# Parameters of a recurrence loaded as contiguous rows and turned into columns by TensorE, and x asked for ahead of the broadcast rows

## The chip, the cores and the metric

One core of a Trainium2 chip runs one program. The metric is the time of the whole program on the device in microseconds (us); lower is better. The kernel before takes 2596.82 us, the median of three runs.

## The reference

Two transformer blocks are computed one after the other for one sequence of 256 tokens with width 1024. The first has three parts that matter here:

```python
ada = silu(c) @ ada_w + ada_b                 # 1024 -> 6144: shifts, scales, gates
h = rms_norm(x, mix_pre_g) * (1 + sc_m) + sh_m
u_s, q, k, v, g_s, g_a = split(h @ w_in)

# the recurrence: 32 groups of 16 channels, 64 complex states each
dt = exp(log_dt)[:, None];  lam_bar = exp(lam * dt)          # lam, dt: (32, 64)
b_bar = ((lam_bar - 1) / lam)[..., None] * b_mat             # (32, 64, 16)
bu = einsum('gpc,sgc->sgp', b_bar, u);  states = scan(lam_bar, bu)
y = einsum('gcp,sgp->sgc', c_mat, states).real + d_skip * u
```

Attention, a mixture of 32 experts and the second block (which also reads a memory whose norm has the gain `mem_norm_2`) follow.

## The kernel before

The kernel is written out by hand for each engine. Every engine has its own program of stages (`pe_s0`, `pe_s1`, ... for TensorE; the same for ScalarE `act_`, VectorE `dve_`, GpSimd `pool_` and SyncE `sp_`) that it runs strictly in order; semaphores connect them. What matters here is stage 0.

**Weights** come through SyncE's DMA queue into a ring of six slots of 2 MB (`RING`, `stream`, L302). The first six pieces are the first half of `ada_w` (1024 x 512 each), then four pieces of `w_in`, then the rest of `ada_w`. `sp_first` asks for c, for the constants `k_main` (identity, masks, tables), for six pieces, and, after waits on `ssm_in` and `rope_in`, for the following ones. From the seventh piece on each waits until TensorE has used the slot.

**Small data** comes through GpSimd's DMA queue (`pool_s0`, L346). The recurrence wants its parameters as columns: state (g, s) of a group pair on one of 128 partitions, the 16 pairs j along the free dimension. So `ssm_lam_re`, `ssm_lam_im` and `ssm_log_dt` (twice) are read by a rearranging access pattern, one 4-byte word at a time; `ssm_d` and `mem_norm_2` likewise; `ssm_b` in runs of 16 words, `ssm_c` in runs of 64 words. Behind these come `positions` spread to all partitions, the table `k_hot` and `rel_bias_2`, then x (1 MB), three rows of `ada_b` and two gains, each spread to 128 partitions (0.5 MB each).

**ScalarE and VectorE** (`act_s0`, `dve_s0`) make silu(c), the rotary tables, and from the parameters `lam_bar` and `bbar`, which is multiplied into block-diagonal masks `Bd` and `Cd`; VectorE then waits (L481) until all six `ada_w` pieces are through TensorE and makes shift, scale and gate (L482 to L486) and h (L572, L573).

**TensorE** (`pe_s0`) waits for silu(c), multiplies it with the six pieces in their order (L507; eight matmuls of 128x128 by 128x512 for a piece, into banks 0 to 5), computes a bias table (`pe_bias`, L335) in bank 7, and transposes `Bd` and `Cd` (L520) into banks 6 and 7. Then it turns h (L553) and starts the projections (L583). A float32 matmul shows as two records in the trace, a transpose as one.

Of the kernel before, what the change touches and what calls it, by code (L numbers as in the profile page):

```python
# [7 lines left out]
P = 128  # L8
# [3 lines left out]
KD = D // P  # L12
# [6 lines left out]
SQ = SW // P  # L19
# [82 lines left out]
def block_kernel(nc, A, out, names):  # L102
# [39 lines left out]
    with ctx:  # L142
# [15 lines left out]
        def ar(at, n, rows=P):  # L158
            return AR[0:rows, at:at + n]
# [76 lines left out]
        def ar3(at, n, k):  # L236
            return ar(at, n).rearrange("p (k m) -> p k m", k=k)
# [11 lines left out]
        braw = [ar3(10240 + 256 * n, 256, SJ) for n in range(2)]  # L249
# [96 lines left out]
        def pool_s0(pool):  # L346
            for s, a in ((lam_re, "ssm_lam_re"), (lam_im, "ssm_lam_im")):
                dma(pool, s, A[a][0].rearrange("(j g) s -> (g s) j", g=2), par_in)
            for g in range(2):
                src = A["ssm_log_dt"][0]  # L350
                dma(pool, dt_c[g * SSM_P:(g + 1) * SSM_P, :],
                    bass.AP(src.tensor, src.offset + g, [[0, SSM_P], [2, SJ]]), par_in)
            for n, a in enumerate(("ssm_b_re", "ssm_b_im")):
                dma(pool, braw[n], A[a][0].rearrange("(j g) s c -> (g s) j c", g=2), ssm_in)
            for n, a in enumerate(("ssm_c_re", "ssm_c_im")):
                dma(pool, craw[n], A[a][0].rearrange("(q r) c s -> (r c) q s", q=SQ), ssm_in)
            dma(pool, dcol, A["ssm_d"][0].rearrange("(q p) -> p q", p=P), ssm_in)
            dma(pool, sinR.bitcast(i32), row(A["positions"][0]), rope_in)
            pool_bias_loads(pool)
            dma(pool, mem_g, A["mem_norm_2"].rearrange("i (k p) -> p i k", p=P), mem_in)  # L360
            dma(pool, x3, A["x"][0].rearrange("(t p) d -> p t d", p=P), x_in)
            for n, d in enumerate((shm, Am, GTm)):
                dma(pool, d, row(A["ada_b"][0][n * D:(n + 1) * D]), mod_in)
            dma(pool, gpre, row(A["mix_pre_g"][0]), mod_in)
            dma(pool, gpost, row(A["mix_post_g"][0]), mod_in)

        def sp_first(sp):

            dma(sp, c_col, A["c"].rearrange("a (k p) -> p (a k)", p=P), c_in)
            dma(sp, CON[:, :], A["k_main"], con_in)  # L370
            stream(sp, 0, SLOTS)
            sp.wait_ge(ssm_in, 16 * 5)
            sp.wait_ge(rope_in, 16)
            stream(sp, SLOTS, FIRST)

        def act_s0(act, o):
            act.wait_ge(c_in, 16)
            o(act.activation(cond, c_col, ACT.Silu), cond_silu)
            act.wait_ge(par_in, 16 * 4)
            o(act.activation(dt_c, dt_c, ACT.Exp), par_exp)  # L380
            act.wait_ge(par_red, 1)
            o(act.activation(mag, mag, ACT.Exp), par_exp)
            act.wait_ge(par_red, 2)
# [8 lines left out]
            for n in range(4):  # L392
                act.wait_ge(bc_ps, n + 1)
                o(act.copy(BC[n], bank(6 + n % 2).rearrange("p (q m) -> p q m", q=SQ)), bc_ev)
# [17 lines left out]
        def dve_s0(dve, o):  # L412
# [4 lines left out]

            dve.wait_ge(rope_in, 16)
# [43 lines left out]
            dve.wait_ge(ssm_in, 16 * 5)  # L462
# [25 lines left out]
        def dve_tables(dve, o):  # L488

            dve.wait_ge(bc_ps, 4)  # L490
# [19 lines left out]
        def pe_s0(pe):  # L510
            pe.wait_ge(cond_ready, 1)
            pe_ada(pe, pc_ada, 0)
            pe_bias(pe)
            for n in range(4):
                pe.wait_ge(bc_ready, n + 1)
                if n >= 2:
                    pe.wait_ge(bc_ev, n - 1)
                src = (Bd + Cd)[n]
                for q in range(SQ):
                    m = pe.transpose(bank(6 + n % 2)[:, q * P:(q + 1) * P], src[:, q * P:(q + 1) * P], ident)  # L520
                m.then_inc(bc_ps, 1)
# [396 lines left out]
        def act_s5(act, o):  # L918
            act_turned(act, o, mgT, "merged")
            act.wait_ge(mem_in, 32)  # L920
# [1258 lines left out]
```

## Time and profile before

| | |
|---|---|
| median of three runs | 2596.82 us (2589.68 to 2599.2) |
| profiled execution, its own time | 2604.98 us |
| span of the profiled execution | 2603.2 us |
| TensorE matmul busy | 2217.3 us (85% of the span), 9934 records |
| VectorE / ScalarE / GpSimd busy | 25% / 14% / 4% |
| mean granted TensorE clock | 0.928 |
| DMA | 580.81 MB, mean 223 GB/s |

The rows further down come from one profiled execution. Times count from the start of its span. "Idle before <- releaser" says how long an engine had done nothing and what ended that. A DMA's "us to landing" counts from the start of its issue. The granted clock is a share of TensorE's full speed, 2.4 GHz; 0.50 is 1.2 GHz. A row with x and a number merges so many records.

### The profile page before, as it was taken

What the parts mean: (1) busy time and instruction counts of PE and PEld (TensorE: products, weight loads), DVE (VectorE), ACT (ScalarE), POOL (GpSimd) and SP (SyncE); (2) the same over time, 40 slices, a digit from 0 to 9 for tenths busy, and PEclk for the clock granted to TensorE, in tenths of its full rate; (3) what the DMA queues carried; (4) which work ended last, traced back from release to release, by engine and by line L of the source; (5) the groups of instructions that cost most, each with busy time, mean ns of one, the idle gap of its engine ahead of it and who ended that gap; (6) DMA issues with size and microseconds to landing.
All of it is one profiled execution on the core that took longest, in us unless ns stands there. A gap on an engine that the chain in (4) does not pass through costs nothing.

```text
span 2603.2 us, 24334 instructions
## 1 busy us (share of the span) xinstructions
PE 2217.3 (85%) x9934; PEld 1222.6 (47%) x9935; DVE 649.2 (25%) x995; ACT 357.7 (14%) x548; POOL 108.2 (4%) x117
## 2 busy tenths in 40 slices
PE   2888689889879999997999887699979776867998
PEld 1554246333223333332333264388638575836873
DVE  2557814111111111110111124200014555421000
ACT  1111011111011111110111111100012221121000
POOL 2000001000000000000000100110000031300000
PEclk9998799999989999998999988899989888888999
DMA  9752235799589999967999862234343300013430
GB/s 224 283 208 78 89 138 228 327 390 428 238 344 428 428 428 428 427 277 329 394 428 427 331 245 81 81 114 145 131 159 102 125 1 1 1 42 115 151 113 16
DMA packets 106898, 580.81 MB, mean 223 GB/s; under 512 B 7123, under 2 KB 8163, under 8 KB 82112
## 3 DMA queue, kind: packets, MB, share of 16 engines
q1 hardware_dynamic: 101008, 562.40, 54.3%
q0 software_dynamic: 5808, 17.19, 2.8%
q8 instruction: 67, 1.10, 0.2%
q14 instruction: 15, 0.12, 0.0%
HBM read 578.49 MB, written 1.07 MB: 223 GB/s over the span
## 4 chain that ended last, share of the span: by engine, by line
PE 70%; DMA 12%; DVE 12%; ACT 4%; issue 3%; SPq 0%; DVEq 0%; another core or an unknown queue 0%; POOL 0%; ACTq 0%
PE ps L1176 15%; PE ps L1482 12%; DMA ring<-in_w_up 10%; PE ps L1192 7%; PE ps L1493 6%; PE ps L583 6%; PE ps L591 5%; PE ps L507 2%; PE ps L1200 2%; DMA ring<-in_ada_w 2%; PE ps L1827 1%; PE ps L1833 1%; PE ps L804 1%; PE ps L1166 1%; PE ps L1837 1%
## 5 line engine op out<-in xcount | busy, mean ns | idle before, releaser
L1176 PE MATMUL ps<-ring,arena 128*64 128x512 f32 x1632 | 365.5, 601 | 43.1 <-issue 30.6
L1482 PE MATMUL ps<-arena,ring 128*128 128x256 f32 x1408 | 308.4, 383 | 1.5 <-ACT arena L560 1.5
L1482 PEld LDWEIGHTS ps<-arena,ring 128*128 128x128 f32 x1408 | 270.2, 192 | 39.7 <-ACT arena L560 2.3
L1176 PEld LDWEIGHTS ps<-ring,arena 128*64 128x64 f32 x1632 | 115.4, 138 | 289.2 <-issue 258.5
L1192 PE MATMUL ps<-ring,arena 128*64 128x512 f32 x1088 | 243.4, 600 | 7.6 <-ACT arena L1135 7.6
L1108 DVE TENSOR_SCALAR arena<-ps 128x512 f32<-128x512 f32 x34 | 23.5, 692 | 614.4 <-PE ps L1176 614.4
L1493 PE MATMUL ps<-ring,arena 128*128 128x512 f32 x352 | 151.4, 592 | 0.0
L583 PE MATMUL ps<-arena,ring 128*128 128x256 f32 x672 | 148.9, 384 | 0.7 <-ACT arena L560 0.7
L1192 PEld LDWEIGHTS ps<-ring,arena 128*64 128x64 f32 x1088 | 75.6, 138 | 152.1 <-issue 137.8
L1176 PE MATMUL ps<-arena 128*64 128x512 f32 x544 | 126.3, 619 | 15.0 <-issue 15.0
L583 PEld LDWEIGHTS ps<-arena,ring 128*128 128x128 f32 x672 | 129.0, 193 | 20.3 <-issue 1.5
L591 PE MATMUL ps<-ring,arena 128*128 128x512 f32 x288 | 130.8, 615 | 3.3 <-ACT arena L1929 2.0
L1493 PEld LDWEIGHTS ps<-ring,arena 128*128 128x128 f32 x352 | 66.9, 190 | 83.3 <-issue 83.2
L553 PE MATMUL ps<-constants,arena 128*128 128x128 f32 x128 | 25.6, 377 | 78.3 <-DVE arena L1439 68.4
L591 PEld LDWEIGHTS ps<-ring,arena 128*128 128x128 f32 x288 | 56.4, 197 | 74.4 <-issue 69.9
L1512 DVE TENSOR_TENSOR arena<-arena,ps 128x512 f32<-128x512 f32 x22 | 15.1, 688 | 302.5 <-ACT arena L1504 302.5
L1176 PEld LDWEIGHTS ps<-arena 128*64 128x64 f32 x544 | 39.2, 142 | 100.3 <-issue 99.5
L507 PE MATMUL ps<-ring,arena 128*128 128x512 f32 x96 | 46.5, 648 | 46.4 <-DMA ring<-in_ada_w 46.4
L1110 DVE TENSOR_SCALAR arena<-ps 128x512 f32<-128x512 f32 x34 | 23.5, 692 | 226.4 <-PE ps L1176 226.4
L1131 ACT ACTIVATE arena<-arena 128x512 f32<-128x512 f32 x34 | 21.5, 632 | 365.9 <-DVE arena L1108 365.9
L532 DVE TENSOR_SCALAR smalls<-smalls 128x2 f32<-128x2 f32 x13 | 2.6, 202 | 266.5 <-ACT arena L526 266.5
L1146 PE MATMUL ps<-arena 128*64 128x512 f32 x280 | 67.9, 606 | 0.0
(445 smaller groups left out, 2166.4 us busy)
## 6 DMA issues: line engine op xcount, KB each, us to landing
ring<-in_w_up SPq DMA_DIRECT2D x64, 2048.0 KB, 17.4
ring<-in_w_down SPq DMA_DIRECT2D x64, 2048.0 KB, 16.6
ring<-in_w_gate SPq DMA_DIRECT2D x32, 2048.0 KB, 14.0
arena<-in_w_gate SPq DMA_DIRECT2D x32, 2048.0 KB, 14.5
ring<-in_ffn_w_gate_up SPq DMA_DIRECT2D x22, 2048.0 KB, 7.9
ring<-in_ada_w SPq DMA_DIRECT2D x12, 2048.0 KB, 19.6
ring<-in_ffn_w_down SPq DMA_DIRECT2D x10, 2048.0 KB, 7.8
ring<-in_w_in SPq DMA_DIRECT2D x8, 2048.0 KB, 19.8
```

The costliest lines, as they stand in the source:

```text
L507: m = pe.matmul(bank(base + n), condrep[:, k, :], w[:, k, :], start=(k == 0), stop=(k == KD - 1))
L583: m = pe.matmul(bank(b0 + c // 2)[:, (c % 2) * SEQ:(c % 2 + 1) * SEQ], w[:, k, c * P:(c + 1) * P], src3[:, k, :], start=(k == 0), stop=(k ...
L591: m = pe.matmul(bank(banks[t]), src3[:, k, t * P:(t + 1) * P], w[:, k, :], start=(k == 0), stop=(k == kn - 1))
L804: m = pe.matmul(bank(b0 + 2 * t + c), src[:, k, t * P:(t + 1) * P], w[:, k, c * 512:(c + 1) * 512], start=(k == 0), stop=(k == 3))
L1146: m = pe.matmul(bank(2)[c * CAP:(c + 1) * CAP, :], Psel[:, t, :], h2[:, t, c * 512:(c + 1) * 512], start=(t == 0), stop=(t == 1))
L1166: pe.matmul(bank(i)[c * CAP:(c + 1) * CAP, :], Ee[odd][i * E:(i + 1) * E, :], bgu[i * E:(i + 1) * E, c * 512:(c + 1) * 512], start=True, s ...
L1176: m = pe.matmul(bank(i)[c * CAP:(c + 1) * CAP, :], xT[:, j * P + h * CAP:j * P + (h + 1) * CAP], w[h][:, j, c * 512:(c + 1) * 512], start= ...
L1192: m = pe.matmul(bank(2)[d * CAP:(d + 1) * CAP, :], actT[:, j * P + h * CAP:j * P + (h + 1) * CAP], down_w[h][:, j, d * 512:(d + 1) * 512], ...
L1200: m = pe.matmul(bank(4 + 2 * t + d), pwT[d * CAP:(d + 1) * CAP, t * P:(t + 1) * P], Yb[d * CAP:(d + 1) * CAP, :], start=False, stop=False, ...
L1482: m = pe.matmul(bank(b0 + g)[:, c * SEQ:(c + 1) * SEQ], w[:, k, (2 * g + c) * P:(2 * g + c + 1) * P], hT2[:, k, :], start=(k == 0), stop=( ...
L1493: m = pe.matmul(bank(2 * t + d), actF[:, f, t * P:(t + 1) * P], w[:, j, d * 512:(d + 1) * 512], start=(f == 0), stop=(f == FC2 - 1))
L1827: m = pe.matmul(bank(b)[:, j * P:(j + 1) * P], scr[:, m_, :], TTm[:, m_, :], start=True, stop=True)
```

## The change

The parameters `lam_re`, `lam_im`, `ssm_d` and `mem_norm_2` are loaded as rows of 128 words into 16, 16, 4 and 16 partitions of one area (`prow`), `log_dt` as 16 rows of two words (`dtrow`), which VectorE widens to rows of 128. TensorE transposes the 68 rows by 128 at once into a corner of bank 6, and VectorE copies the columns to where the kernel before had them. `ssm_b` is loaded as 16 rows of 2048 words for the real and the imaginary part; TensorE turns each of the 16 channels by a transpose of 16 x 128, for both 32 transposes, into banks 6 and 7, where VectorE reads them in place of `braw`. They stand on TensorE between the second and the third piece of `ada_w`. `positions` and x are asked for ahead of `k_hot`; waits are renumbered.

```diff
--- before.py
+++ after.py
@@ -246,7 +246,10 @@
         cosS, sinS = ar3(10240, 4096, SJ), ar3(14336, 4096, SJ)
         BTr, BTi, CTr, CTi = (ar3(18432 + 512 * n, 512, SQ) for n in range(4))
 
-        braw = [ar3(10240 + 256 * n, 256, SJ) for n in range(2)]
+        brow = [ar(14336 + 2048 * n, 2048, SJ) for n in range(2)]
+        PR = {"lam_re": 0, "lam_im": SJ, "dt": 2 * SJ, "d": 3 * SJ, "mem_g": 3 * SJ + SQ}
+        PROWS = 3 * SJ + SQ + 2 * KD
+        prow, dtrow = ar(11008, P, PROWS), AR[PR["dt"]:PR["dt"] + SJ, 11136:11138]
         bbar = [ar3(10752 + 256 * n, 256, SJ) for n in range(2)]
         craw = [ar3(11264 + 256 * n, 256, SQ) for n in range(2)]
         btmp = ar3(11776, 256, SJ)
@@ -344,21 +347,18 @@
 
 
         def pool_s0(pool):
-            for s, a in ((lam_re, "ssm_lam_re"), (lam_im, "ssm_lam_im")):
-                dma(pool, s, A[a][0].rearrange("(j g) s -> (g s) j", g=2), par_in)
-            for g in range(2):
-                src = A["ssm_log_dt"][0]
-                dma(pool, dt_c[g * SSM_P:(g + 1) * SSM_P, :],
-                    bass.AP(src.tensor, src.offset + g, [[0, SSM_P], [2, SJ]]), par_in)
+            for n, a in (("lam_re", "ssm_lam_re"), ("lam_im", "ssm_lam_im")):
+                dma(pool, prow[PR[n]:PR[n] + SJ, :], A[a][0].rearrange("(j g) s -> j (g s)", g=2), par_in)
+            dma(pool, dtrow, A["ssm_log_dt"][0].rearrange("(j g) -> j g", g=2), par_in)
+            dma(pool, prow[PR["d"]:PR["d"] + SQ, :], A["ssm_d"][0].rearrange("(q p) -> q p", p=P), par_in)
+            dma(pool, prow[PR["mem_g"]:PR["mem_g"] + 2 * KD, :], A["mem_norm_2"].rearrange("i (k p) -> (i k) p", p=P), par_in)
+            dma(pool, sinR.bitcast(i32), row(A["positions"][0]), rope_in)
             for n, a in enumerate(("ssm_b_re", "ssm_b_im")):
-                dma(pool, braw[n], A[a][0].rearrange("(j g) s c -> (g s) j c", g=2), ssm_in)
+                dma(pool, brow[n], A[a][0].rearrange("(j g) s c -> j (g s c)", g=2), ssm_in)
             for n, a in enumerate(("ssm_c_re", "ssm_c_im")):
                 dma(pool, craw[n], A[a][0].rearrange("(q r) c s -> (r c) q s", q=SQ), ssm_in)
-            dma(pool, dcol, A["ssm_d"][0].rearrange("(q p) -> p q", p=P), ssm_in)
-            dma(pool, sinR.bitcast(i32), row(A["positions"][0]), rope_in)
+            dma(pool, x3, A["x"][0].rearrange("(t p) d -> p t d", p=P), x_in)
             pool_bias_loads(pool)
-            dma(pool, mem_g, A["mem_norm_2"].rearrange("i (k p) -> p i k", p=P), mem_in)
-            dma(pool, x3, A["x"][0].rearrange("(t p) d -> p t d", p=P), x_in)
             for n, d in enumerate((shm, Am, GTm)):
                 dma(pool, d, row(A["ada_b"][0][n * D:(n + 1) * D]), mod_in)
             dma(pool, gpre, row(A["mix_pre_g"][0]), mod_in)
@@ -369,18 +369,18 @@
             dma(sp, c_col, A["c"].rearrange("a (k p) -> p (a k)", p=P), c_in)
             dma(sp, CON[:, :], A["k_main"], con_in)
             stream(sp, 0, SLOTS)
-            sp.wait_ge(ssm_in, 16 * 5)
+            sp.wait_ge(ssm_in, 16 * 4)
             sp.wait_ge(rope_in, 16)
             stream(sp, SLOTS, FIRST)
 
         def act_s0(act, o):
             act.wait_ge(c_in, 16)
             o(act.activation(cond, c_col, ACT.Silu), cond_silu)
-            act.wait_ge(par_in, 16 * 4)
+            act.wait_ge(par_red, 1)
             o(act.activation(dt_c, dt_c, ACT.Exp), par_exp)
-            act.wait_ge(par_red, 1)
+            act.wait_ge(par_red, 2)
             o(act.activation(mag, mag, ACT.Exp), par_exp)
-            act.wait_ge(par_red, 2)
+            act.wait_ge(par_red, 3)
             o(act.activation(lbi, frq, ACT.Sin, scale=TWO_PI))
             o(act.activation(lbr, tc, ACT.Sin, scale=TWO_PI), par_trig)
             act.wait_ge(rope_red, 1)
@@ -390,7 +390,7 @@
             act_rms(act, o, [x3[:, t, :] for t in range(TT)], hT[:, 0:4, :].rearrange("p k m -> p (k m)"), 1)
             act_bias(act, o)
             for n in range(4):
-                act.wait_ge(bc_ps, n + 1)
+                act.wait_ge(bc_ps, n + 3)
                 o(act.copy(BC[n], bank(6 + n % 2).rearrange("p (q m) -> p q m", q=SQ)), bc_ev)
 
         def act_tables(act, o, h):
@@ -415,6 +415,13 @@
             o(dve.tensor_copy(condrep, cols_bc(cond, P)))
             o(dve.tensor_copy(cond32, cols_bc(cond, 32)), cond_ready)
 
+            dve.wait_ge(par_in, 16 * 5)
+            o(dve.tensor_copy(prow[PR["dt"]:PR["dt"] + SJ, :].rearrange("j (g s) -> j g s", g=2), cols_bc(dtrow, SSM_P)), bc_ready)
+            dve.wait_ge(bc_ps, 1)
+            prT_ = bank(6)[:, SJ * SSM_C:SJ * SSM_C + PROWS]
+            o(dve.tensor_copy(sm(16, 3 * SJ), prT_[:, 0:3 * SJ]), par_red)
+            o(dve.tensor_copy(dcol, prT_[:, PR["d"]:PR["d"] + SQ]))
+            o(dve.tensor_copy(sm(1136, 2 * KD), prT_[:, PR["mem_g"]:PR["mem_g"] + 2 * KD]), bc_ready)
             dve.wait_ge(rope_in, 16)
             dve.wait_ge(con_in, 16)
             o(dve.tensor_copy(cosR, sinR.bitcast(i32)))
@@ -459,7 +466,9 @@
             o(dve.tensor_tensor(tc2, lbr, lam_im, ALU.mult))
             o(dve.tensor_tensor(ci, ci, tc2, ALU.subtract))
             o(dve.tensor_tensor(ci, ci, den, ALU.mult))
-            dve.wait_ge(ssm_in, 16 * 5)
+            dve.wait_ge(bc_ps, 2)
+            dve.wait_ge(ssm_in, 16 * 4)
+            braw = [bank(6 + n)[:, 0:SJ * SSM_C].rearrange("p (c j) -> p j c", c=SSM_C) for n in range(2)]
             crb, cib = cols_bc(cr, SSM_C), cols_bc(ci, SSM_C)
             o(dve.tensor_tensor(bbar[0], braw[0], crb, ALU.mult))
             o(dve.tensor_tensor(btmp, braw[1], cib, ALU.mult))
@@ -487,7 +496,7 @@
 
         def dve_tables(dve, o):
 
-            dve.wait_ge(bc_ps, 4)
+            dve.wait_ge(bc_ps, 6)
             steps = spread(con("steps"), [0, 4], [1, SEQ])
             for h in range(4):
                 f3, t3 = sinS[:, 4 * h:4 * h + 4, :], cosS[:, 4 * h:4 * h + 4, :]
@@ -508,11 +517,23 @@
                 m.then_inc(ada_ps, 1)
 
         def pe_s0(pe):
+            pe.wait_ge(con_in, 16)
+            pe.wait_ge(bc_ready, 1)
+            pe.transpose(bank(6)[:, SJ * SSM_C:SJ * SSM_C + PROWS], prow, ident[0:PROWS, 0:PROWS]).then_inc(bc_ps, 1)
             pe.wait_ge(cond_ready, 1)
-            pe_ada(pe, pc_ada, 0)
+            pe_ada(pe, pc_ada[0:2], 0)
+            pe.wait_ge(ssm_in, 16 * 4)
+            pe.wait_ge(bc_ready, 2)
+            for n in range(2):
+                by_c = brow[n].rearrange("j (s c) -> j c s", c=SSM_C)
+                for c in range(SSM_C):
+                    m = pe.transpose(bank(6 + n)[:, c * SJ:(c + 1) * SJ], by_c[:, c, :], ident[0:SJ, 0:SJ])
+            m.then_inc(bc_ps, 1)
+            pe_ada(pe, pc_ada[2:6], 2)
+            pe.wait_ge(bc_ready, 3)
             pe_bias(pe)
             for n in range(4):
-                pe.wait_ge(bc_ready, n + 1)
+                pe.wait_ge(bc_ready, n + 3)
                 if n >= 2:
                     pe.wait_ge(bc_ev, n - 1)
                 src = (Bd + Cd)[n]
@@ -917,7 +938,7 @@
 
         def act_s5(act, o):
             act_turned(act, o, mgT, "merged")
-            act.wait_ge(mem_in, 32)
+            act.wait_ge(mem_in, 16)
             act_rms(act, o, [mem_nat[:, t, :] for t in range(TT)], ar(10240, D), 2)
             act_turned(act, o, mem_T[0], "memory")
             act.wait_ge(out_ps, 5)
```

## Rows read from the trace of the kernel before

**Rows 1.** The page's chain that ended last, by line.

```profile
PE ps L1176 15%; PE ps L1482 12%; DMA ring<-in_w_up 10%; PE ps L1192 7%; PE ps L1493 6%; PE ps L583 6%; PE ps L591 5%; PE ps L507 2%; PE ps L1200 2%; DMA ring<-in_ada_w 2%; PE ps L1827 1%; PE ps L1833 1%; PE ps L804 1%; PE ps L1166 1%; PE ps L1837 1%
```

**Rows 2.** The chain in order of time, 0 to 420 us: start, us, what.

```profile
1.84 42.44 DMA ring<-in_ada_w
44.41 10.15 PE ps L507 x16
...
56.59 36.31 PE ps L507 x80
...
107.19 44.06 PE ps L583 x192
```

**Rows 3.** Timeline, 92 to 104 us: start, us, instruction, idle before.

```profile
93.02 1.22 DVE L482 TENSOR_TENSOR arena<-arena,ps 128x1024 f32<-128x1024 f32 x1 [35.73 <-PE ps L507]
...
95.81 1.09 PE L520 MATMUL ps<-constants,arena 128*128 128x128 f32 x8 [1.96 <-ACT arena L343]
...
97.26 0.42 PEld L520 LDWEIGHTS ps<-constants,arena 128*128 128x128 f32 x4 [0.59 <-issue]
...
101.91 1.97 PE L553 MATMUL ps<-constants,arena 128*128 128x128 f32 x8 [3.37 <-DVE arena L573]
```

**Rows 4.** Windows of the start: busy us by engine, PEclk, DMA share, GB/s.

```profile
9.00:18.00 9.00, 0.00 (x0) 0.00 (x0) 0.00 (x0) 0.00 (x0) 7.24 (x12) 1.00 0.98 6
18.00:22.00 4.00, 0.00 (x0) 0.00 (x0) 0.00 (x0) 0.00 (x0) 0.00 (x0) 1.00 1.73 38
22.00:29.00 7.00, 0.00 (x0) 0.00 (x0) 0.00 (x0) 0.00 (x0) 0.00 (x0) 1.00 0.31 85
29.00:38.00 9.00, 0.00 (x0) 0.00 (x0) 0.00 (x0) 1.50 (x2) 0.00 (x0) 1.00 1.14 214
38.00:45.00 7.00, 0.59 (x1) 0.50 (x2) 5.91 (x24) 1.14 (x2) 0.00 (x0) 1.00 1.03 378
```

**Rows 5.** DMA issues, 0 to 150 us: count, KB each, us to landing.

```profile
constants<-in_k_main SPq DMA_DIRECT2D x1, 1265.0 KB, 7.5
...
x_res<-in_x POOLq DMA_DIRECT2D x1, 1024.0 KB, 32.2
...
arena<-in_mix_post_g POOLq DMA_DIRECT2D x1, 512.0 KB, 39.5
...
arena<-in_ssm_b_im POOLq DMA_DIRECT2D x1, 128.0 KB, 25.7
...
arena<-in_ssm_c_im POOLq DMA_DIRECT2D x1, 128.0 KB, 26.3
...
smalls<-in_ssm_lam_im POOLq DMA_DIRECT2D x1, 8.0 KB, 11.3
```

**Rows 6.** Timeline of GpSimd's queue: start and us of the issue.

```profile
1.24 1.32 POOL L295 DMA_DIRECT2D smalls<-in_ssm_lam_re  x1 [0.81 <-POOLq L2167]
...
3.71 1.78 POOL L295 DMA_DIRECT2D smalls<-in_ssm_log_dt  x2
...
6.63 1.15 POOL L295 DMA_DIRECT2D arena<-in_ssm_b_im  x1
...
12.83 0.73 POOL L295 DMA_DIRECT2D x_res<-in_x  x1
...
15.70 0.54 POOL L295 DMA_DIRECT2D arena<-in_mix_post_g  x1
```

**Rows 7.** The two loads of in_ssm_log_dt, by tile.

```profile
DMA to landing us min/median/max: 15.8/20.3/24.9
```

**Rows 8.** DMA queues, 38 to 45 us (q1 is SP's, q0 GpSimd's).

```profile
q0 software_dynamic: 464, 1.72, 65.8%
q1 hardware_dynamic: 469, 0.93, 37.6%
```

**Rows 9.** Windows: two stretches at low clock, columns as in rows 4.

```profile
58.00:61.40 3.40, 3.40 (x6) 1.24 (x6) 0.00 (x0) 0.00 (x0) 0.00 (x0) 0.59 1.05 384
...
102.00:107.00 5.00, 3.84 (x16) 3.04 (x16) 4.86 (x5) 2.22 (x4) 0.00 (x0) 0.50 0.97 360
```

## The prediction

> **What bounds the kernel now.** I read the chain that ended last by line first [rows 1]. It is mostly matmuls, and the DMA in it splits in two: the expert weights `w_up` (10% of the span), which the change does not touch, and 2% for `ada_w`. So I read the chain in order of time for its start [rows 2]. There the reader sees four things in a row: 42.4 us in which everything waits for the first 2 MB piece of `ada_w`, 10.15 us of TensorE for that piece (8 matmuls, each recorded twice), 36.3 us for the other five pieces, and, 14.2 us after those end at 92.9, the first projection at 107.2. All that follows hangs on this chain one after the other. The end of the six `ada_w` pieces is therefore the point to move: the modulation on VectorE (L482) waited 35.7 us for it and nothing else [rows 3].
>
> Why does a 2 MB piece asked for at 1.84 us land at 44.3? The windows answer it [rows 4]. From 9 to 29 us the DMA engines move 6, 38 and 85 GB/s, together 0.8 MB in 20 us, although two pieces of `ada_w` are queued on SP's side all along. After it they move 214, then 378 GB/s. What holds them is to be read from the landings [rows 5] and the issues [rows 6]: `k_main`, asked for just ahead of `ada_w`, lands 7.5 us later, at about 9; `ssm_lam_im`, issued at 1.24 + 1.32 = 2.56, at 13.9; and the two loads of `ssm_log_dt`, issued from 3.7 on, 15.8 and 24.9 us after their issues [rows 7], at 19.5 and 29.6. Each of these (with `ssm_lam_re` four) writes 128 x 16 single words to 128 partitions, each word from an address of its own: 8,192 pieces of 4 bytes, 512 for each of 16 engines, in about 25 us (the issue at 1.24, some 3 us until data moves, the end at 29.6), or 49 ns apiece. Then `b_im` lands at 6.63 + 25.7 = 32.3, `c_im`, two issues later, at about 35, x at 45.0, and the last row of the queue, `mix_post_g`, at 15.70 + 39.5 = 55.2. So GpSimd's queue and SP's queue share the engines, and words crawling in one starve the other.
>
> **What the change removes.** Gone are the 8,192 words above, 512 words of `ssm_d` and 2,048 of `mem_norm_2` (at 49 ns on 16 engines 1.6 and 6.3 us), and 4,096 runs of 64 bytes of `ssm_b` (at most the 2.7 us between 29.6 and 32.3). In their place come rows of 512 bytes (68 rows less the 16 of `dt`, which are 8 bytes each and widened on VectorE) and 32 rows of 8 KB. That is 0.3 MB in a few hundred pieces: about 1 us at 378 GB/s. The `ssm_c` loads, 256-byte runs, stay; b, c and `positions` are 0.65 MB.
>
> **When the first piece lands then (S).** No row shows it. Lower bound: after `k_main` at about 9, the piece alone at 378 GB/s takes 5.5 us, S = 14. Upper bound if the words are really gone: all of GpSimd's 4.6 MB (x 1.05, five spread rows 2.6, `k_hot` 0.2, b, c and `positions` 0.65, small rows) and both queued pieces (4.2 MB) come first, 8.8 MB / 0.378 = 23.3, S = 32. Between them decides how the two queues share. While x and the broadcast rows flowed (38 to 45 us), SP's queue got 0.93 of 2.65 MB, 35% [rows 8], or 0.133 MB a us. GpSimd's issues now come sooner: x was issued at 12.83, loads of single words or short runs ahead of it costing up to 1.3 us each (1.32, 1.15); whole rows cost 0.54 [rows 6], so x is asked for at about 7 and flows from about 10. Until then SP's queue gets about half, 0.4 MB. Then 1.7 MB remain; at 0.133 they take 12.8 us (S = 23), and up to 3 us more because pieces land with their slowest engine. I take S = 24, by the sharing row, between the bounds; 19 to 29 is its likely spread.
>
> One rule of the Trainium skill speaks against the new form (SBUF — State Buffer, the DMA port swizzle): neighbouring partitions share a port, in fours, so rows that fill only 16 partitions reach 4 of 16 ports. By it the 0.26 MB of b, at a sixteenth of 435 GB/s per port, would be an estimated 2.4 us instead of 0.7, S = 26 and the time 2579. No row here shows a load of 16 partitions; the trace can't judge it.
>
> **What it adds.** (1) One transpose of 68 x 128 on TensorE ahead of `ada_w`, four small copies and one widening copy on VectorE. TensorE stands at it for the five row loads, and `ada_w` is queued behind. They are at the head of the queue where two loads of words took until 13.9, so I put them at 8 to 12, hidden by the wait for S; if S were below 12 it would cost the difference. (2) 32 transposes of 16 x 128 between the second and the third piece of `ada_w`, in line on TensorE. Eight transposes of 128 x 128 take 1.09 us at full clock and 1.97 at granted clock 0.5; the weight loads alone take 0.42 for four [rows 3, 9]. Bounds: 32 x 0.105 = 3.4 and 32 x 0.246 = 7.9. I take 32 x 0.136 = 4.3, since 128 columns are loaded for each either way and TensorE is then in full run. The price is on the path. TensorE also waits there for b and c and for VectorE's copies; by my sum it arrives at S + 17 = 41, they at 15. (3) VectorE's bbar work waits for these transposes, S + 21 = 45, and takes the 6 us it takes now, done by 52, where the modulation will wait until 73. Slack 21 us. Behind it stand the mask products, which TensorE asks for after piece 6.
>
> Moving x, `k_hot` and the `mem_norm_2` rows changes nobody's last wait: all land before TensorE's last piece. SP's waits on `ssm_in` and `rope_in` are met before slot 0 comes free. DMA supply of the pieces: two are through when GpSimd's queue is empty (about 25), the second by 31 against S + 10 = 34; the others follow every 5.5 us against 6.9 on TensorE, so the sixth is there at 53. With that the 2.0 us stall between 54.6 and 56.6 goes [rows 2], and with it, I assume, the half clock of 58.0 to 61.4 (granted 0.59) that followed it [rows 9], 1.2 GHz in place of 2.4, worth half of 3.4, 1.7 us.
>
> **Sum.** End of `ada_w` = 24 + 10.15 + (36.3 - 1.7) + 4.3 = 73.1 against 92.9: 19.8 us less. From there all waits are on engines or on ring slots that TensorE frees, so the gain is carried to the end. Profiled execution: 2605.0 - 19.8 = 2585.2. It was 8.2 above the median of the runs; against that median 2596.8 - 19.8 = 2577.
>
> **Rivals.** (a) *The larger part of the delay stays*: SP's piece goes on waiting behind the megabytes that GpSimd now asks for sooner, or the 16-partition rows are slow. S = 31 to 36 gives 2584 to 2589. For: pieces did not get more than a third beside x [rows 8]. Against: at 378 GB/s the 4.6 MB and one piece are through by 27. (b) *The piece comes nearly alone*: GpSimd's data starts later than I think, S = 14 to 18, 2567 to 2571. For: a queue whose loads take some time to begin leaves the engines to the other, and the large loads might begin late. Against: x asked for at 7 is early. (c) *The start is gained and lost again*: small transposes, or later waits, put TensorE at half clock; four pieces behind the transposes at half clock cost up to 27 us, an end at 100, 2604, no measurable change. For: half clock after only 2 us of idling [rows 9]. Against: transposes leave TensorE hardly idle. It could also be lost in the expert stage, where the chain waits for `w_up` [rows 1]; but its slots are freed by TensorE, so the asking moves too. (d) *Slower*: TensorE, in order, stands before the 32 transposes for the fourth of b and c. If that lands at T, the end is T + 4.3 + 27.3; nothing is left from T = 61, and over 0.5% is lost from T = 74. Before, `c_im` landed at 34.8 behind 8,192 words; it would have to get later by 40 us with the words gone. (e) *The words were not what held the engines* (a slow start of the queue itself): S stays above 36, within 0.5%. Against: `b_re` and `b_im`, with 4,096 larger pieces, passed in 2.7 us directly behind them.
>
> **How the numbers follow.** Forecast 0.60, (a) 0.14, (b) 0.10, (c) 0.07, (d) 0.03, (e) 0.06. A measurement of this kernel can tell about 0.5%, 13 us; the three runs before span 9.5 us. The likeliest case alone (S of 19 to 29) runs from 2572 to 2582. Taking in (b) and (a) gives 2566 to 2590. Faster by over 0.5% means below 2583.8: the forecast, (b), and a fifth of (a), 0.73, less what scatter takes: 0.72. Within 0.5%: 0.25. Slower: 0.03.
>
> **What would show it.** Right: the DMA windows from 9 to 29 us carry over 300 GB/s; TensorE's first `ada_w` matmul starts at 19 to 29, runs to about 73 with the 32 transposes as 4 to 5 us in it, no idle time after piece 1; L482 starts there; the first projection 14 us later; GpSimd's queue is empty by about 25. Wrong: first matmul later than 31; TensorE idle ahead of the transposes; granted clock under 0.9 between the transposes and the sixth piece; an interval between L482 and the end of the span that has grown by more than 5 us.

## The result, and the profile after

The changed kernel takes 2617.94 us (median of 17 runs, 2608.0 to 2643.18), the kernel before 2602.18 beside it (17 runs, 2589.68 to 2608.94): 1.0077, 95% interval [1.0058, 1.0096]. It is slower by 0.8%, where 0.8% faster was forecast. Ratios here and below come from the executions within 1.5% of the fastest of the same kernel (three of e1's twelve and one of e6's six are left out of theirs), so they are not quotients of the medians. The profiled execution took 2634.42, its span is 2632.6 against 2603.2, 29.4 us more.

The start first. TensorE's timeline of the kernel after, 12 to 75 us:

```profile
22.58 10.11 PE L516 MATMUL ps<-ring,arena 128*128 128x512 f32 x16 [12.89 <-DMA ring<-in_ada_w]
33.96 7.13 PE L516 MATMUL ps<-ring,arena 128*128 128x512 f32 x16 [1.27 <-DMA ring<-in_ada_w]
41.03 3.69 PE L530 MATMUL ps<-constants,arena 16*128 16x16 f32 x32
44.65 29.43 PE L516 MATMUL ps<-ring,arena 128*128 128x512 f32 x64
```

VectorE's timeline of the same run, the modulation that L482 was before:

```profile
74.22 1.22 DVE L491 TENSOR_TENSOR arena<-arena,ps 128x1024 f32<-128x1024 f32 x1 [21.74 <-PE ps L516]
```

Windows of the start after, columns as in rows 4, the last one just behind the 32 transposes:

```profile
9.00:18.00 9.00, 0.35 (x1) 0.18 (x1) 5.89 (x24) 1.74 (x4) 2.63 (x6) 1.00 1.00 254
18.00:22.00 4.00, 0.00 (x0) 0.00 (x0) 2.63 (x15) 3.65 (x7) 0.00 (x0) 1.00 1.06 315
22.00:29.00 7.00, 6.42 (x8) 2.71 (x9) 0.88 (x5) 1.17 (x3) 0.00 (x0) 1.00 1.03 398
44.70:49.00 4.30, 4.30 (x8) 1.74 (x8) 3.93 (x8) 0.00 (x0) 0.00 (x0) 0.62 1.04 387
```

Against [rows 3, 4] the reader sees the start do what the change is for: 254 to 398 GB/s where there were 6 to 85, and L491 at 74.22 where L482 stood at 93.02, 18.8 us earlier. (The prediction's sign was over 300 GB/s in all of 9 to 29 us; the first window stays under it.) VectorE carries this to the door of the expert stage, first the kernel after, then before, the same operation of its timeline:

```profile
400.75 1.28 DVE L1064 SCALAR_TENSOR_TENSOR arena<-x_res,smalls,arena 128x1024 f32<-128x1024 f32 x1
```

```profile
419.19 1.28 DVE L1043 SCALAR_TENSOR_TENSOR arena<-x_res,smalls,arena 128x1024 f32<-128x1024 f32 x1
```

So 18.4 us are still in hand at 400 us, and 29.4 are missing at the end: 47.8 us were lost behind it, in code that the diff does not touch. Where? The groups of TensorE's instructions by line, from 400 us on, after and then before (lines stand 21 lower there; busy and mean, then idle time and its releasers):

```profile
L1197 PE MATMUL ps<-ring,arena 128*64 128x512 f32 x1632 | 372.2, 606 | 61.9 <-issue 53.2 <-DMA ring<-in_w_up 8.3
L1213 PE MATMUL ps<-ring,arena 128*64 128x512 f32 x1088 | 244.1, 602 | 7.6 <-ACT arena L1156 7.6
L1197 PE MATMUL ps<-arena 128*64 128x512 f32 x544 | 138.8, 640 | 36.4 <-issue 36.4
```

```profile
L1176 PE MATMUL ps<-ring,arena 128*64 128x512 f32 x1632 | 365.5, 601 | 43.1 <-issue 30.6 <-DMA ring<-in_w_up 12.0
L1192 PE MATMUL ps<-ring,arena 128*64 128x512 f32 x1088 | 243.4, 600 | 7.6 <-ACT arena L1135 7.6
L1176 PE MATMUL ps<-arena 128*64 128x512 f32 x544 | 126.3, 619 | 15.0 <-issue 15.0
```

The counts are the same, and so is the down projection (L1213). The gate and up projection (L1197) is idle 98.3 us where it was 58.1, and "issue" makes up 44.0 of that growth, while the wait for `w_up` shrank by 3.7. It is busy 19.2 us longer too. "Issue" means that the engine waited for no semaphore that the profile shows. The waits of TensorE from 420 to 1940 us count these stops (us in total, times, longest), after, then before:

```profile
PE ps L1197 <- issue: 89.6, 14, 14.1
```

```profile
PE ps L1176 <- issue: 45.6, 6, 12.6
```

So the kernel before has such stops too, at 487 and 523 us in the loop's first pass, and at 701, 734, 1184 and 1226 behind the only two further rounds. (TensorE's loop computes two experts in a pass; an expert with more tokens than one round holds gets a further round, whose code is jumped over otherwise.) The timeline says when the new ones come. After, TensorE from 1100 to 1165 us:

```profile
1100.31 1.99 PE L1221 MATMUL ps<-arena 64*128 64x512 f32 x8
1116.37 16.19 PE L1197 MATMUL ps<-ring,arena 128*64 128x512 f32 x64 [14.07 <-issue]
...
1144.36 1.99 PE L1221 MATMUL ps<-arena 64*128 64x512 f32 x8
1151.16 3.24 PE L1197 MATMUL ps<-arena 128*64 128x512 f32 x6 [4.82 <-issue]
1156.64 5.74 PE L1197 MATMUL ps<-arena 128*64 128x512 f32 x25 [2.24 <-issue]
```

The same point of the loop in the kernel before, one expert and the next:

```profile
1118.28 1.99 PE L1200 MATMUL ps<-arena 64*128 64x512 f32 x8
1120.20 7.09 PE L1176 MATMUL ps<-arena 128*64 128x512 f32 x32
...
1147.69 1.99 PE L1200 MATMUL ps<-arena 64*128 64x512 f32 x8
```

Between two combines (L1200, L1221) lie 29.4 us before and 44.1 after. TensorE stands still between the end of one expert and the first matmul of the next, where the loop jumps (back to its top, or over the code of a further round that is not taken). One queue has more to do in the whole execution, and part of that in this gap. The queues, whole execution, after, then before (packets, MB, share):

```profile
q8 instruction: 84, 1.38, 0.2%
```

```profile
q8 instruction: 67, 1.10, 0.2%
```

Each packet is 16 KB. Ahead of the loop they come about every 256 records of TensorE, so they are the fetches of its instructions, 256 to a block. From 1095 to 1165 us the kernel after has nine, four of them between 1104 and 1113; the kernel before has one from 1100 to 1165. Going by the records at which TensorE loads each expert's count, the kernel before takes 998.3 us from the first load to the last and the kernel after 1054.1. Two groups of two experts make up 41 us of it: 44.2 + 37.6 us where the kernel before took 35.3 + 27.7, and 44.0 + 37.1 where it took 29.4 + 29.4, so 19 and 22 us a group. The other 15 us lie at the experts where the kernel before stops as well, and the kernel after for longer (39.3, 39.4 and 40.0 us against 35.7, 33.6 and 34.8 at the largest three). The loss in the loop, 55.8, less 8.0 given back behind it, is the 47.8. These 8 us need no cause in the change: from the last count load to the end the profiled executions of all kernels here take between 1108.0 and 1124.5 us, 1119.9 before and 1112.0 after.

The theory then (T1): the 69 instructions that the change adds to TensorE's program ahead of the loop (33 transposes, each a weight load and a matmul, and three waits) move the loop against the blocks of 256, and at some places a jump's target has to be fetched while the engine stands. The rivals: (T2) the loss is in the data, because x and the expert weights meet other traffic; (T3) it is scatter between programs of this length, whatever is in them.

### The profile page after: what moved, and what is told of

Same layout as the page of the kernel before. It is cut to its first block, busy times and chain, and to the rows that moved or that the text cites. A ratio compares the mean times of both kernels' runs of the same rounds, so it can differ in the third digit from the quotient of the medians.

```text
span 2632.6 us, 24408 instructions
## 1 busy us (share of the span) xinstructions
PE 2232.1 (85%) x9967; PEld 1234.4 (47%) x9968; DVE 649.0 (25%) x999; ACT 357.2 (14%) x548; POOL 103.9 (4%) x116
## 4 chain that ended last, share of the span: by engine, by line
PE 70%; DVE 12%; DMA 9%; issue 4%; ACT 4%; SPq 0%; DVEq 0%; POOL 0%; ACTq 0%
PE ps L1197 16%; PE ps L1503 12%; DMA ring<-in_w_up 8%; PE ps L1213 7%; PE ps L1514 6%; PE ps L604 6%; PE ps L612 5%; PE ps L1221 2%; PE ps L1848 1%; PE ps L516 1%; PE ps L1854 1%; DMA ring<-in_ada_w 1%; PE ps L825 1%; PE ps L1187 1%; PE ps L1858 1%
## 5 line engine op out<-in xcount | busy, mean ns | idle before, releaser
L1197 PE MATMUL ps<-ring,arena 128*64 128x512 f32 x1632 | 372.2, 606 | 61.9 <-issue 53.2
L1197 PEld LDWEIGHTS ps<-ring,arena 128*64 128x64 f32 x1632 | 121.4, 140 | 305.4 <-issue 283.6
L1213 PE MATMUL ps<-ring,arena 128*64 128x512 f32 x1088 | 244.1, 602 | 7.6 <-ACT arena L1156 7.6
L1197 PE MATMUL ps<-arena 128*64 128x512 f32 x544 | 138.8, 640 | 36.4 <-issue 36.4
L1514 PE MATMUL ps<-ring,arena 128*128 128x512 f32 x352 | 151.4, 592 | 0.0
L1213 PEld LDWEIGHTS ps<-ring,arena 128*64 128x64 f32 x1088 | 75.8, 138 | 152.4 <-issue 138.3
L612 PE MATMUL ps<-ring,arena 128*128 128x512 f32 x288 | 129.0, 608 | 3.3 <-ACT arena L1950 2.0
L1197 PEld LDWEIGHTS ps<-arena 128*64 128x64 f32 x544 | 44.2, 145 | 129.0 <-issue 128.2
L612 PEld LDWEIGHTS ps<-ring,arena 128*128 128x128 f32 x288 | 55.8, 195 | 73.3 <-issue 68.8
L1167 PE MATMUL ps<-arena 128*64 128x512 f32 x280 | 71.8, 606 | 0.0
L1221 PE MATMUL ps<-arena 64*128 64x512 f32 x272 | 67.6, 615 | 0.0
## 6 DMA issues: line engine op xcount, KB each, us to landing
ring<-in_w_in SPq DMA_DIRECT2D x8, 2048.0 KB, 18.8
```

The costliest lines, as they stand in the source:

```text
L612: m = pe.matmul(bank(banks[t]), src3[:, k, t * P:(t + 1) * P], w[:, k, :], start=(k == 0), stop=(k == kn - 1))
L1167: m = pe.matmul(bank(2)[c * CAP:(c + 1) * CAP, :], Psel[:, t, :], h2[:, t, c * 512:(c + 1) * 512], start=(t == 0), stop=(t == 1))
L1197: m = pe.matmul(bank(i)[c * CAP:(c + 1) * CAP, :], xT[:, j * P + h * CAP:j * P + (h + 1) * CAP], w[h][:, j, c * 512:(c + 1) * 512], start= ...
L1213: m = pe.matmul(bank(2)[d * CAP:(d + 1) * CAP, :], actT[:, j * P + h * CAP:j * P + (h + 1) * CAP], down_w[h][:, j, d * 512:(d + 1) * 512], ...
L1221: m = pe.matmul(bank(4 + 2 * t + d), pwT[d * CAP:(d + 1) * CAP, t * P:(t + 1) * P], Yb[d * CAP:(d + 1) * CAP, :], start=False, stop=False, ...
L1514: m = pe.matmul(bank(2 * t + d), actF[:, f, t * P:(t + 1) * P], w[:, j, d * 512:(d + 1) * 512], start=(f == 0), stop=(f == FC2 - 1))
```

## Experiments

Each group of runs had the kernel before beside it (medians 2601.71, 2603.11, 2602.28, 2605.23 and 2601.37); the ratio is against those.

**e1 to e3: empty instructions at the head of TensorE's program.** In the changed kernel 187, in the kernel before 69 and 128:

```diff
         def pe_s0(pe):
+            for _ in range(187):
+                pe.nop(nofuse=True)
```

> The changed kernel with 187 empty instructions at the head of TensorE's program, where it idles for data anyway. With the 69 instructions that the change added this makes 256, so TensorE's expert loop lies as in the kernel before against blocks of 256 instructions (16 KB). Theory (place of the loop against the fetched blocks costs the stalls): the 18.8 us of the start are kept, stalls as before, about 2583, 67 instruction fetches. Rival (the change itself slows the expert stage, through DMA phase, memory placement or clock): about 2618, as the changed kernel, 84 fetches.

> The kernel before with 69 empty instructions at the head of TensorE's program, nothing else. Theory: the expert stage gets the changed kernel's stalls without its gain, 2602 + 34 = about 2636 and over 80 fetches. Rival: 2602, 67 fetches.

> The kernel before with 128 empty instructions at TensorE's head, half a block. Theory: another place of the loop and so another time, anything from 2580 to 2650, with the number of instruction fetches going along with it. Rival: 2602.

Measured: e1 2614.13, 1.0011 [0.9975, 1.0048]; e2 2601.89, 1.0003 [0.9988, 1.0018]; e3 2602.49, 1.0006 [0.9989, 1.0023]. These say nothing on T1: e1 has 24408 instructions like the kernel after, and its fetches come at about the same records. TensorE has 2560 records ahead of the loop's first in the kernel before and also in e2 and e3, and 2629 in the kernel after and also in e1; the empty instructions never reached the engine. But e1 thereby shows the changed kernel again: its 12 runs lie between 2589.0 and 2677.4, and its profiled run has 77 fetches and one extra group (45.2 + 37.7 us) where the kernel after had two. The loss comes in portions and differs from run to run. The same kernel before, with 35 runs beside it, spans 2592.3 to 2611.49.

**e4: x ahead of the broadcast rows, alone, in the kernel before.**

```diff
+            dma(pool, x3, A["x"][0].rearrange("(t p) d -> p t d", p=P), x_in)
             pool_bias_loads(pool)
             dma(pool, mem_g, A["mem_norm_2"].rearrange("i (k p) -> p i k", p=P), mem_in)
-            dma(pool, x3, A["x"][0].rearrange("(t p) d -> p t d", p=P), x_in)
```

> The kernel before with x alone asked for ahead of the table and the spread rows; no parameter load is changed and no TensorE instruction is added. My step says that x is nobody's last wait: 2602. If the order of the loads on GpSimd's queue made the later loss, it would be above 2610.

Measured 2599.46, 1.0003 [0.9985, 1.002], 67 fetches. The move of x does neither good nor harm; the first `ada_w` matmul starts at 45.36. T2 in the form "x's traffic" is out.

**e5, e6: real instructions as padding.** The changed kernel with 94 small transposes (187 more in its instruction count), which with the change's 69 puts its loop 256 instructions, one block, behind that of the kernel before; and the kernel before with 34 (68 more), which puts its loop within one instruction of where the changed kernel has it. The traces agree: 2816 and 2628 records ahead of the loop's first, 256 and 68 more than before. The edit of e5:

```diff
             pe.wait_ge(con_in, 16)
+            for _ in range(94):
+                pe.transpose(bank(7)[0:16, 0:16], ident[0:16, 0:16], ident[0:16, 0:16])
```

> The empty instructions of the runs before never reached TensorE (its instruction fetches came at the same places), so those runs padded nothing. Here 94 transposes of 16x16 with their weight loads (187 more instructions) stand at TensorE's head in the changed kernel, in its idle time: with the change's 69 a whole block of 256. Theory (place of the expert loop against the fetched blocks): no extra groups of instruction fetches, 2583 and a spread as narrow as before's. Rival (timing alone, the loop's place does not matter): median near 2615, spread from 2590 to 2675.

> 34 such transposes at TensorE's head in the kernel before (68 instructions, as many as the change adds within one), nothing else. Theory: extra groups of instruction fetches at 25 us each, a median of 2610 to 2640 and a wide spread. Rival: 2602, 67 fetches.

Measured: e5 2587.61, 0.9941 [0.9927, 0.9956], 68 fetches; e6 2647.93, 1.0183 [1.0153, 1.0214]. The kernel before became slower by 1.8% through work that ends long before `ada_w` arrives, and the changed kernel became faster than the kernel before through adding work. T2 can't do that, as the loads are the same, nor can T3, with intervals this far from 1. e6's profiled run was its fastest (2618.41) and shows 68 fetches and, beyond the stops that the kernel before has, three of about 2 us (51.6 us in nine), 1012.5 us from the first count load to the last; its slower runs have no trace, so that their 19 to 43 us more were lost in such stops is not shown.

**e7, e8: the loop's place set by an alignment directive,** in the changed kernel, nothing else changed. For e8 the second number is 128; all later kernels "at N" are this edit with N:

```diff
             pe_open(pe, 0)
+            pe.addr_align(256, 0, 0)
             expert_rounds(pe, first, lambda e, odd, r, n: pe_further(pe, e, odd, n))
```

Measured: 2588.13, 0.9945 [0.9929, 0.9961], and 2588.68, 0.9942 [0.9926, 0.9958], 69 fetches each. The groups of e8, the same lines as above:

```profile
L1197 PE MATMUL ps<-ring,arena 128*64 128x512 f32 x1632 | 365.5, 601 | 43.2 <-issue 31.1
...
L1197 PE MATMUL ps<-arena 128*64 128x512 f32 x544 | 128.0, 623 | 15.2 <-issue 15.2
```

Busy and idle times are those of the kernel before, its 46 us of stops included. With the loop put elsewhere, what the change gains at the start arrives at the end. That the two places would differ, as I had expected of e8, did not come true.

**e9, e10: the place that I took for the bad one.** The loop at 192 in the changed kernel and in the kernel before.

> The changed kernel with TensorE's expert loop at place 192 of its block. If 69 instructions more turn good places into a bad one and 0 and 128 are good, the bad stretch should lie between 128 and 256. Theory: bad, 2605 to 2650 and wide, 75 or more instruction fetches. Rival (a directive just ahead of the loop cures it, at any place): 2588 and narrow, as at 0 and 128.

> The kernel before with the same directive and place 192, nothing of the change in it. Theory: bad too, 2620 to 2660, as the run with 34 added transposes. Rival: 2602.

Measured: 2586.07, 0.9944 [0.9922, 0.9967], and 2606.4, 1.0009 [0.9992, 1.0026], 67 fetches each. My expectation missed: 192 is harmless. This left open whether a bad place exists at all or the directive cures the loop by its presence.

**e13 to e17: the places between.** The changed kernel at 144, 160, 176 and 152, and the kernel before at 160.

> The changed kernel, loop at place 144. By the record numbers at which the fetches fall, the changed kernel's own place lies at 144 to 190. Theory (a bad stretch between 128 and 192): at least one of 144, 160 and 176 is slow and wide, 2605 to 2650. Rival (the directive cures at any place): 2587.

> The same at place 160. Theory: the likeliest of the three to be slow, 2605 to 2650, 75 or more instruction fetches. Rival: 2587.

> The same at place 176. Theory: slow, 2605 to 2650, if the bad stretch reaches so far; rival: 2587.

> The kernel before, loop at place 160. Theory: the same answer as the changed kernel at 160, 19 us later: 2620 to 2665 if that is slow. Rival: 2602.

> The changed kernel, loop at place 152. Theory (the changed kernel's own place lies on a slope between 144 and 160): between 2603 and 2946, with a wide spread, 75 to 187 instruction fetches. Rival (a step at 160 alone): 2603 as at 144, or 2585.

Measured:

| kernel, loop at | us | against before | fetches |
|---|---|---|---|
| after, 144 | 2603.03 (2586.87 to 2610.79) | 0.998 [0.9962, 0.9998] | 72 |
| after, 152 | 2935.11 (2929.86 to 2938.05) | 1.1277 [1.1258, 1.1296] | 187 |
| after, 160 | 2945.77 (2944.34 to 2951.45) | 1.1303 [1.1289, 1.1318] | 187 |
| after, 176 | 2584.47 (2582.87 to 2589.86) | 0.9925 [0.9912, 0.9938] | 67 |
| before, 160 | 2962.8 (2957.64 to 2970.83) | 1.1378 [1.1362, 1.1393] | 187 |

Nothing but the loop's place differs, and the time goes up by some 360 us in both kernels; the directive cures nothing by itself. I had expected 160 to be slow, but by 20 to 60 us; 176 to be slow, where it is free; and 152 to lie between with a wide spread, where it is nearly as slow as 160 and its five runs span 8 us. The page of the kernel at 160:

```profile
q8 instruction: 187, 3.06, 0.5%
...
PE 70%; issue 14%; DVE 11%; ACT 3%; DMA 2%; DVEq 0%; POOL 0%; SPq 0%; ACTq 0%
...
L1197 PE MATMUL ps<-ring,arena 128*64 128x512 f32 x1632 | 388.9, 636 | 192.3 <-issue 192.3
...
L1197 PE MATMUL ps<-arena 128*64 128x512 f32 x544 | 153.7, 729 | 178.4 <-issue 178.4
```

and its timeline over one expert:

```profile
636.09 1.99 PE L1221 MATMUL ps<-arena 64*128 64x512 f32 x8
649.04 8.99 PE L1197 MATMUL ps<-arena 128*64 128x512 f32 x32 [10.97 <-issue]
...
676.71 1.99 PE L1221 MATMUL ps<-arena 64*128 64x512 f32 x8
```

Nearly every expert now looks as the two groups of the kernel after did: 31 stops of "issue", all but one of 10 to 14 us, 40.6 us from combine to combine here and up to 43.9 elsewhere, 120 more fetches in the whole execution (eight to ten in each pass of the loop). The kernel before at 160 has 368.2 us of stops, also 31; the changed kernel at 152 has 331.6 in 47, one long stop and two short ones for two experts. The idle time of L1197 is 370.7 us against 98.3 after and 58.4 at 128. The matmuls that follow a stop are slower as well (8.99 us for 32 where the kernel before takes 7.09; the mean granted clock of the execution is 0.879 against 0.92 after), and the DMA's share of the chain falls from 9% to 2%: the weights, which used to be awaited, are there.

**Where the loops without a directive stand** can be read from the traces. Behind the loop the code runs straight on, so the number of TensorE's records from the last fetch to the end of the program goes with the place. It is 100, 228, 244, 252, 260, 276 and 292 for the places 0, 128, 144, 152, 160, 176 and 192, the last and 260 in both kernels: always the place plus 100. It is 176 in the kernel before, e2 to e5 included, 246 in the kernel after and e1, and 244 in e6. That puts the loop at 76, 146 and 144, give or take two. With it all profiled executions fall in line (from the first count load to the last):

| place | runs | us in the loop |
|---|---|---|
| 0 | e7 | 1006.6 |
| 76 | before, e2, e3, e4, e5 | 994.5 to 1000.7 |
| 128 | e8, e11, e12 | 999.2 to 1002.8 |
| 144 | e6, e13 | 1012.5, 1014.2 |
| 146 | after, e1 | 1054.1, 1026.9 |
| 152 | e17 | 1346.7 |
| 160 | e14, e16 | 1363.3, 1361.0 |
| 176 | e15 | 1001.6 |
| 192 | e9, e10 | 998.1, 998.8 |

So the change moved the loop by 69 instructions from a free place, 76, to the lower edge of the stretch that costs.

**e11, e12: what of the start could be had more cheaply.** Both with the loop at 128. e11 leaves `ssm_b` loaded as before, in 64-byte runs, without the 32 transposes; e12 moves them and their waits ahead of `ada_w`:

```diff
-                dma(pool, brow[n], A[a][0].rearrange("(j g) s c -> j (g s c)", g=2), ssm_in)
+                dma(pool, braw[n], A[a][0].rearrange("(j g) s c -> (g s) j c", g=2), ssm_in)
...
-            for n in range(2):
-                by_c = brow[n].rearrange("j (s c) -> j c s", c=SSM_C)
...
```

```diff
-            pe.wait_ge(cond_ready, 1)
-            pe_ada(pe, pc_ada[0:2], 0)
             pe.wait_ge(ssm_in, 16 * 4)
...
             m.then_inc(bc_ps, 1)
+            pe.wait_ge(cond_ready, 1)
+            pe_ada(pe, pc_ada[0:2], 0)
```

> The changed kernel, loop at 128, with ssm_b loaded as before in runs of 64 bytes and without the 32 transposes: the 4-byte words alone are gone. My step puts b's short runs at 2.7 us at most and the transposes, by the profile after, at 3.7: first ada_w matmul at 22 to 26 us, the end of ada_w no later than with b turned, 2585 to 2589. Rival (b's runs carry a large part of the 20 us): first matmul at 30 or later, 2595.

> The changed kernel, loop at 128, with the 32 transposes ahead of the first piece of ada_w, in TensorE's wait for it. b and c are there at 16.4 us by the profile after and the piece at 22.5, so the 3.7 us leave the path, and TensorE may be at full clock for the first piece (10.1 us there, 7 at full clock). Expected 2588.7 less 3.7 to 6.9: 2582 to 2585. Rival (the first piece then waits for the transposes, or the clock falls back): no gain, 2588.

Measured: e11 2585.21, 0.9932 [0.9907, 0.9958]; e12 2580.63, 0.9918 [0.9892, 0.9945]. TensorE's timeline of e12:

```profile
15.89 3.71 PE L528 MATMUL ps<-constants,arena 16*128 16x16 f32 x32 [6.36 <-DMA arena<-in_ssm_c_im]
22.90 8.58 PE L516 MATMUL ps<-ring,arena 128*128 128x512 f32 x16 [3.31 <-DMA ring<-in_ada_w]
34.48 34.60 PE L516 MATMUL ps<-ring,arena 128*128 128x512 f32 x80 [2.99 <-DMA ring<-in_ada_w]
```

and of e11:

```profile
21.82 8.79 PE L514 MATMUL ps<-ring,arena 128*128 128x512 f32 x16 [12.95 <-DMA ring<-in_ada_w]
34.35 36.30 PE L514 MATMUL ps<-ring,arena 128*128 128x512 f32 x80 [3.74 <-DMA ring<-in_ada_w]
```

The short runs of b cost nothing, so the gain is that of the single words; and early transposes are hidden, `ada_w` ending at 69.1, 5.0 us sooner than after. In all three the second piece is there only at 34, so that is what bounds the start next: the second piece's landing. e12 is the fastest kernel of the study, 0.82% under the kernel before, and its interval does not quite part it from e11's or e8's.

## Why the prediction was wrong

**Step by step.** The first piece, S: 24 taken, 22.58 measured, inside the likeliest spread. The share of SP's queue was a fair guide but low (42% of the bytes moved from 8.2 to 22.6 us, where the row had 35%), the last row of GpSimd's queue landed at 32.6 and not by 25, and the five row loads landed before 9 us, ahead of S as said. The 32 transposes: 4.3 taken, 3.69 measured, hence 0.115 us each, and they found b and c there (`c_im` landed by 16.4), so rivals (a), with its slow 16-partition rows, and (d) fell: `b_re` and `b_im` landed 7.9 and 8.9 us after their issues, the 256-byte runs of c behind them 9.5 and 9.9. (e11, with b spread over 128 partitions again, has its first piece 0.9 us before e8; one execution of each can't say whether b's 16 rows cost that.) The end of `ada_w`: 73.1 taken, 74.08 measured. Behind S, 1.4 better than said, and the transposes, 0.6 better, the other five pieces and their stall took 37.8 us where 34.6 stood. Two effects that I let go are there: the stall ahead of the second piece (1.27 us; 3.0 in e12 and 3.7 in e11, where the first piece is done sooner), because the second piece lands at about 34, not by 31; and a stretch at granted clock 0.62 (44.7 to 49.0 us) that follows, now behind the transposes, one of the signs that the prediction had named. So the start gained 18.8 us where 19.8 stood.

**The step that failed** is the sentence "From there all waits are on engines or on ring slots that TensorE frees, so the gain is carried to the end". It was true up to 400 us (18.4 left), and it left out a thing that TensorE waits for without a semaphore: its own instructions. With it failed the costing of the added instructions: I priced the 32 transposes where they run, 3.7 us, and not by what 69 more instructions do to the place of all that follow. That priced them at nothing in the expert loop, which took 55.8 us more in the profiled run. The prediction's own sign for it came true: from L482 (L491 after) to the end of the span it is 2558.4 us instead of 2510.2, 48.2 more, where more than 5 was to count as wrong.

**What is shown.** The loop's place alone moves the kernel between 2584 and 2946 us (e7, e8, e9, e15 against e14, e17), with the same work and the same loads. It does so in the kernel before too (e16), where e10 at 192 costs nothing. 68 instructions added ahead of the loop in the kernel before make it slower by 1.8% (e6), and 187 more in the changed kernel take it from 0.8% slower to 0.6% faster (e5). The stop is at the jumps, in "issue", with fetches of code beside it (84 and 187 against 67 to 69). The start by itself is worth what was forecast, less a little: changed kernels with a harmless place lie at 2584 to 2589, 14 to 21 us under the kernel before beside them, against 19.8 forecast.

The Trainium skill has the rule for this (Runtime: NRT & Kernel Launch, Instruction fetch mechanics): instructions come in 16 KB blocks of 256, and a taken branch whose target lies outside the current window of two blocks makes the engine wait for a fetch. The traces agree with the block's size, 16 KB to a packet, and with the wait at the jump. They do not agree with a window of two: a pass of the loop has 551 records, more than two blocks, and the kernel before runs from 768.7 to 1154.5 us, over ten experts, without one fetch. The page gives no price for the wait; here a stop is 10 to 14 us at most, 19 and 22 us a group.

**My rivals.** (c), gained and lost again in the expert stage, was the one that came true in place, at 0.07, but not in mechanism: I looked for it in `w_up`, and the wait for `w_up` got shorter. It also ended on the far side of no change, which no case of mine but (d), at 0.03, did; none had the code's place in it.

**What stays open.** At 144 to 146 the loss comes in portions that are there in one run and not in the next: at 144 the runs spread over 24 us (e13) and 43 (e6), the kernel after's over 35, e1's over 88. What sets off a portion was not found. Why 152 and 160 are bad at every expert and 144 and 176 nearly or wholly free is not settled either, nor is why the two further rounds bring stops at every place: it needs the number of blocks that the engine holds and which it gives up first, and no run here shows those. Why the first piece takes 8.6 to 8.8 us of TensorE in e8, e11 and e12 and 10.1 after was not tested; the granted clock is 1.00 over it in e8, e12 and after alike, so the rows of the clock do not tell them apart.

## What to carry to other kernels

An edit that adds or removes instructions of an engine moves every loop behind it against the blocks in which its code is fetched, so look at the "issue" rows and the instruction queue's packets of each such loop before and after, and read or fix the place of a long loop (here 0, 128, 176 or 192 of 256) before you judge the edit by its time. Single 4-byte words loaded on one queue hold up megabytes on another: look for windows with a full queue and a few GB/s, and load rows and transpose them instead. Put the transposes where the engine waits anyway (e12), not between two pieces of its path.

## What the runs showed of the hardware that was not expected

- The place of a loop of TensorE in the 256-instruction blocks is worth between nothing (0, 128, 176, 192) and 350 to 360 us of 2600 (152 and 160), 14% at most. Eight instructions (144 to 152) decide over 332 us of it. The kernels here had stood at 76 and, changed, at 146.
- At a place on the edge the loss comes in portions (19 and 22 us in the kernel after, two experts each), in some executions and not in others, so that one kernel's runs spread over 88 us (e1) where its neighbours spread over 10 to 20.
- A fetch's packet itself takes 0.9 to 2.2 us; the engine's stops at a jump were 2 to 6 and 10 to 14 us long. Even the kernels at a free place have 45 to 47 us of them, in the first pass and behind the two further rounds.
- 32 transposes of 16 x 128 take 3.69 us, 0.115 each, about the 0.105 that a weight load alone took before [rows 3].
